# Causal attention on one core: the mask moves from TensorE products to the VectorE pass that takes the row maximum

## What is computed

```
q, kc, vc, ks, vs, kw, vw, gl = split(h @ w_in)      # 16 heads in 4 groups, head size 64
sc = q @ k_cmp.T ; p_c = softmax(where(valid_c, sc, -1e30))        # compressed keys (31)
ss = q @ ks.T    ; p_s = softmax(where(key_pos <= t_pos, ss, -1e30))  # selected blocks
sw = q @ kw.T    ; p_w = softmax(where(rel >= 0,         sw, -1e30))  # window of 512
o  = g0 * (p_c @ v_cmp) + g1 * (p_s @ vs) + g2 * (p_w @ vw)
out = o @ w_out
```

## Time and profile before

| | |
|---|---|
| time, median of 3 runs | 2454.04 us (2453.34 to 2454.38) |
| time of the profiled execution | 2452.17 us |
| span of the profiled execution | 2450.4 us, so 1.8 us lie around it |
| TensorE busy | 2412.6 us (98%) |
| VectorE busy | 1308.5 us (53%) |
| ScalarE busy | 884.7 us (36%) |
| TensorE clock granted | 0.996 of full speed |

### The profile page before, as it was taken

The page is one execution under the profiler, slowest core; times in us unless marked ns, Lnnn a source line. Parts: engine busy times, 40 slices in busy tenths (PEclk is TensorE's granted clock), DMA queues, the critical chain, the costliest instruction groups (busy, mean ns, idle before and its releaser), DMA issues.

```text
span 2450.4 us, 33828 instructions
## 1 busy us (share of the span) xinstructions
PE 2412.6 (98%) x12064; PEld 2015.1 (82%) x12064; DVE 1308.5 (53%) x1868; ACT 884.7 (36%) x1366; POOL 326.3 (13%) x314
## 2 busy tenths in 40 slices
PE   8999999999999999999999999999999999999998
PEld 6888888888888888888888888888888888888887
DVE  7656655444355655343487544446655665534444
ACT  5257753223234333222333322223336773322222
POOL 4311122000012030000033000003410114000003
PEclk9999999999999999999999999999999999999999
DMA  4810003232323223223232323233650002223232
GB/s 143 213 63 1 1 27 103 94 103 86 103 94 120 86 93 104 95 94 103 91 107 95 104 87 102 94 103 103 163 164 10 1 1 78 94 95 103 88 101 85
DMA packets 67480, 220.38 MB, mean 90 GB/s; under 512 B 7600, under 2 KB 11824, under 8 KB 67376
## 3 DMA queue, kind: packets, MB, share of 16 engines
q1 hardware_dynamic: 61680, 208.89, 25.8%
q0 software_dynamic: 5120, 8.39, 1.7%
q10 hardware_dynamic: 576, 1.69, 0.2%
HBM read 208.46 MB, written 2.10 MB: 86 GB/s over the span
## 4 chain that ended last, share of the span: by engine, by line
PE 93%; DVE 4%; ACT 1%; issue 1%; DMA 1%; DVEq 0%; SPq 0%; ACTq 0%
PE bank L1361 89%; PE bank L1583 3%; ACT attn L709 1%; DVE big L1260 1%; DVE w_lo L850 1%; DVE xs_lo L858 0%; DVE nmax L1098 0%; DMA raw<-stream 0%; ACT w_hi L525 0%; PE bank L1613 0%; DMA par<-params 0%; DVE big L1253 0%; DVE tmp L1221 0%; DVE big L1354 0%; DVE branch L1120 0%
## 5 line engine op out<-in xcount | busy, mean ns | idle before, releaser
L1361 PE MATMUL bank<-xs_hi,w_hi 128*128 128x512 f32 x1808 | 712.4, 394 | 7.4 <-DVE xs_lo L858 7.0
L1361 PE MATMUL bank<-xs_hi,w_lo 128*128 128x512 f32 x1808 | 704.6, 390 | 0.0
L1361 PE MATMUL bank<-xs_lo,w_hi 128*128 128x512 f32 x1808 | 704.5, 390 | 0.0
L850 DVE TENSOR_TENSOR w_lo<-raw,w_hi 128x1024 fp32r<-128x1024 f32 x372 | 471.2, 1270 | 242.8 <-ACT w_hi L525 238.4
L525 ACT ACTIVATE w_hi<-raw 128x1024 fp32r<-128x1024 f32 x373 | 391.8, 1051 | 432.1 <-PE bank L1361 257.2
L1361 PEld LDWEIGHTS bank<-xs_hi,w_hi 128*128 128x128 f32 x1808 | 339.9, 188 | 83.5 <-DVE xs_lo L858 8.1
L1361 PEld LDWEIGHTS bank<-xs_lo,w_hi 128*128 128x128 f32 x1808 | 340.1, 188 | 70.9 <-issue 1.9
L1361 PEld LDWEIGHTS bank<-xs_hi,w_lo 128*128 128x128 f32 x1808 | 339.9, 188 | 71.1
L1361 PE MATMUL bank<-hid_hi,w_hi 128*128 128x512 f32 x720 | 280.6, 390 | 0.0
L1361 PE MATMUL bank<-hid_lo,w_hi 128*128 128x512 f32 x720 | 280.1, 389 | 0.0
L1361 PE MATMUL bank<-hid_hi,w_lo 128*128 128x512 f32 x720 | 280.1, 389 | 0.0
(11 more groups left out here) (190 smaller groups left out, 2718.9 us busy)
## 6 DMA issues: line engine op xcount, KB each, us to landing
raw<-stream SPq DMA_DIRECT2D x371, 512.0 KB, 3.3
w_f<-stream SPq DMA_DIRECT2D x18, 512.0 KB, 4.0
hid_hi<-mix_hi POOLq DMA_DIRECT2D x32, 128.0 KB, 6.7
hid_lo<-mix_hi POOLq DMA_DIRECT2D x32, 128.0 KB, 6.7
x<-x_in SPq DMA_DIRECT2D x8, 256.0 KB, 8.6
out<-big SPq DMA_DIRECT2D x8, 256.0 KB, 3.5
raw<-stream ACTq DMA_DIRECT2D x2, 512.0 KB, 7.7
work<-b_s ACTq DMA_DIRECT2D x1, 512.0 KB, 5.0
```

Source lines behind the costliest of these rows:

```text
L850: nc.vector.tensor_tensor(w_lo[:, slot, :], raw[:, k, :], f32(w_hi[:, slot, :]), ALU.subtract).then_inc(w_lo_ready, counted(b))
L1361: return nc.tensor.matmul(out_, w, v, start=start, stop=stop)
```

## The change

The constant `causal_b` grows from 128 to 512 columns: 384 zeros and then the 128 by 128 triangle of -1e30, so that its last w columns are the mask of a unit of w columns. The mask products go. `maximum` of a causal pack becomes one instruction a unit that reads the scores from PSUM and the mask from SBUF, writes -(score + mask) to `prob` and takes its minimum, which is the negated maximum, into `nmax`. The exponents then read `prob` in place with scale -1. `scores(p)` waits for `max_ready` of pack p-2, no longer for its `prob_ready`. The wait for `prob_t` of pack p-4 moves from ScalarE to VectorE.

```diff
@@ exponents (ScalarE)
-                        wait_past(act, prob_t, p0 + p - 3)
                         for j in range(n):
-                            last = nc.scalar.activation(prob[:, p % 4, bass.ts(j, w)], bank[p % 2][:, bass.ts(j, w)],
-                                                        ACT.Exp, bias=nmax[:, p % 4, j:j + 1])
+                            sc = prob[:, p % 4, bass.ts(j, w)]
+                            last = nc.scalar.activation(sc, sc, ACT.Exp, bias=nmax[:, p % 4, j:j + 1], scale=-1.0)
@@ maximum (VectorE)
-                        sc = bank[p % 2][:, 0:pack_width(p)]
-                        nc.vector.tensor_reduce(nmax[:, p % 4, 0:n], sc.rearrange("p (j w) -> p j w", j=n), AX.X,
-                                                ALU.max, negate=True).then_inc(max_ready, 1)
+                        w = P * (t_of(i) + 1)
+                        wait_past(dve, prob_t, p0 + p - 3)
+                        for j in range(n):
+                            last = nc.vector.tensor_tensor_reduce(
+                                out=prob[:, p % 4, bass.ts(j, w)], in0=bank[p % 2][:, bass.ts(j, w)],
+                                in1=causal_b[:, S - w:S], scale=-1.0, scalar=-NEG, op0=ALU.add, op1=ALU.min,
+                                accum_out=nmax[:, p % 4, j:j + 1])
+                        last.then_inc(max_ready, 1)
@@ scores (TensorE)
-                    wait_past(pe, prob_ready, p0 + p - 1)
+                    wait_past(pe, max_ready, p0 + p - 1)
...
-                            mm(both, q, key_hi[:, :, g, 0:P], j == 0, False)
-                            mm(both, q, key_lo[:, :, g, 0:P], False, False)
-                        last = mm(dst[:, :].rearrange("p (k w) -> p k w", k=4), ident_b[:, :],
-                                  causal_b[:, :].unsqueeze(1).broadcast_to([P, 4, P]), False, True)
+                            mm(both, q, key_hi[:, :, g, 0:P], True, False)
+                            last = mm(both, q, key_lo[:, :, g, 0:P], False, True)
...
-                            mm(dst[:, bass.ts(k, w)], q, key_lo[:, br, g, 0:w], False, False)
-                            last = mm(dst[:, bass.ts(k * (t + 1) + t, P)], ident_b[:, :], causal_b[:, :], False, True)
+                            last = mm(dst[:, bass.ts(k, w)], q, key_lo[:, br, g, 0:w], False, True)
```

More of the change, by code:

```diff
@@ L85 @@
 PAR_COLS = _at
-CON = {"ident": 0, "causal": 128, "tril": 256, "cmask": 384, "end": 384 + TT * P}
+CON = {"ident": 0, "causal": P, "tril": P + S, "cmask": 2 * P + S, "end": 2 * P + S + TT * P}
 CON_COLS = CON["end"]
@@ L239, in build @@
         ident_b = sb("ident_b", [P, P], BF16)
-        causal_b = sb("causal_b", [P, P], BF16)
+        causal_b = sb("causal_b", [P, S], BF16)
         cmask_b = sb("cmask_b", [P, TT, P], BF16)
@@ L807, in _ @@
                                  ).then_inc(con_ready, 1)
-            nc.scalar.activation(causal_b[:, :], con[:, CON["causal"]:CON["causal"] + P], ACT.Copy
+            nc.scalar.activation(causal_b[:, :], con[:, CON["causal"]:CON["causal"] + S], ACT.Copy
                                  ).then_inc(con_ready, 1)
@@ L1840, in _consts @@
     con[:, CON["ident"]:CON["ident"] + P] = np.eye(P)
-    con[:, CON["causal"]:CON["causal"] + P] = np.where(r[None, :] > r[:, None], NEG, 0.0)
+    con[:, CON["causal"] + S - P:CON["causal"] + S] = np.where(r[None, :] > r[:, None], NEG, 0.0)
     con[:, CON["tril"]:CON["tril"] + P] = (r[None, :] >= r[:, None])
```

## The result

The changed kernel takes 2436.7 us (2435.5 to 2437.5, 4 runs) against 2453.7 before: ratio 0.9932, 95% interval 0.9915 to 0.995.

The account below looks back on a forecast made before the run. TensorE, busy 98% of the span, was taken to bound the kernel. Terms -13.8 (masks) + 2.4 (chain) + 0.6 (stall) + 2.8 (t1) = -8.0 us gave 2446.0 us, range 2440 to 2463.

Parts of the forecast that it names:

- a: VectorE's new fixed cost per unit, for the second instruction of a pass that writes `nmax`: taken as 0.08 us.
- the overlap: On VectorE, an instruction that waits for nothing starts 0.08 us before the end of the one before it.
- my lower bound of 0.013: Lowest fixed cost per unit considered, 0.013 us, from the companion instruction of the shuffle; the upper bound was 0.167.
- the 16 units: Units per group in which VectorE's fixed cost counts: 8 in the chain, one in the stall, about 7 others; 128 in all.
- my own formula: Sum of -8.0 us, moved by 1.3 us for each 0.01 us of fixed cost per unit; gain gone at 0.14.
- Masks: Mask products leaving TensorE: 7.7 us in t3 and t2 plus 6.1 in t1, so 13.8 us saved outside the chain.
- The chain at the group's end: Two t0 packs going round all three engines, TensorE waiting for exponents: 0.3 us longer, 2.4 us in 8 groups.
- The earlier wait: `scores` waits for `max_ready` alone, so its 0.6 us lie beside the exponents; otherwise the chain is 0.9 longer.
- The stall on `normalize_cs`: TensorE's wait for VectorE's normalization, some 6 us after the group's end: 0.08 us longer, 0.6 us in 8 groups.
- t1's loss of 0.35 a group: VectorE's extra 0.32 us in each of four t1 packs, a little over one showing: 0.35 a group, 2.8 us.
- The exponents from SBUF: ScalarE's exponents reading SBUF instead of PSUM: 0.03 us more an instruction, mattering for four in a row in t0.
- The rival that hung on the rule: Slower: no overlap between a pass and its second instruction, t0 units spaced 0.46 us, +14 us, 2468 us; chance 0.22.

Follow-up runs that it names:

- e2: Changed kernel with one more tiny VectorE copy of one column ahead of each of the 256 passes: 2447.48 us, ratio to before 0.9979.
- e3: Changed kernel with two tiny VectorE copies ahead of each pass: 2456.53 us, ratio to before 1.0021.
- e5: Kernel before without its mask products, nothing else changed, so its attention is not causal: 2438.15 us, ratio to before 0.9937.
- e1: Changed kernel with scores(p) waiting for `prob_ready` of pack p-2 again instead of `max_ready`: 2444.97 us, ratio to before 0.9963.
- e8: Changed kernel with both VectorE reorderings, `normalize_cs` of t0 items ahead of the maximum and `out_low` one step later: 2423.42 us, ratio to before 0.9884.
- e7: Changed kernel with `out_low` one step later on VectorE, behind the next maximum: 2429.82 us, ratio to before 0.9913.
- e6: Changed kernel with `normalize_cs` of the t0 items ahead of the maximum of the same step on VectorE: 2431.03 us, ratio to before 0.9921.
- e4: Changed kernel with the mask products put back on TensorE, so the mask is added twice: 2453.48 us, ratio to before 1.0012.

## Why the prediction was wrong

**The step that failed: "I take a = 0.08".** It was worked out as "0.167 - 0.08", a tiny pass less the overlap. Measured, a is 0.00 (the timeline above), below even my lower bound of 0.013. Two things were wrong in it. A tiny copy costs 0.06 where it stands ahead of each pass, not 0.08 (e2 and e3), which is a small matter. And the read of the accumulator is not like a tiny pass: it starts 0.08 us before the end of its own pass, and the next pass starts together with it, so that it delays nothing. I had taken one overlap off its duration, when it lies under its own pass as a whole.

**The size that this makes.** With the 13 units of e2 and e3, a = 0.08 would have made the group 43.48 + 13 x 0.08 = 44.5 us, an estimate, so 1.0 a group or 8 us in all below before: the forecast's 8.0. The sum came out right for the a that I put in, but in part by luck: the 16 units were too many, and the masks were worth more than I gave them (below). With a = 0 my own formula, -8.0 - 128 x 0.08, gives -18.2; with 13 units a group, 104 in all, -16.3. Measured are -16.3 by groups and -17.0 by the medians.

The group, cut at the chain's two ends (us, change against before; the e5 column has no mask and the old pass):

| part | forecast | changed | e5 |
|---|---|---|---|
| chain, last `lo` product of the first t0 pack to the transposes of the second | +0.30 | -0.25 | -0.24 |
| rest of the t3 item, with the stall | -0.40 | -0.48 | -0.64 |
| t2 item | -0.48 | -0.62 | -0.62 |
| t1 item | -0.41 | -0.76 | -0.58 |
| start of the t0 item to that `lo` product | 0 | +0.08 | 0 |
| sum | -0.99 | -2.03 | -2.08 |

Of the 1.04 us between forecast and measurement, the rows that hang on a (chain, rest of t3, t1) make up 0.55 + 0.08 + 0.35; the masks of the t2 item bring 0.14 more and the t0 start takes 0.08 back.

**Point by point.**
- Masks: forecast 13.8 us outside the chain, measured 16.6 in all (e5). In the timeline of the changed kernel the distance from the `lo` product to the transposes in t3 is what was forecast:

```profile
205.44 0.40 PE L1365 MATMUL bank<-hid_lo,mix_hi 128*128 128x512 f32 x1
205.68 0.38 PE L1584 MATMUL bank<-ident,attn 128*128 128x128 f32 x2
```

  0.24 us, against 0.30 before. Over a whole item a mask is worth a little more than these 0.06: t2's eight packs won 0.62, so 0.08 each. Of t1, 8.15 us became 7.39, so 0.19 for each of 4 packs, as forecast. Of t0's two masks the first one shortens the chain by its 0.23, which the forecast had in it (e5: 0.24). The second is not won: in e5 the chain is

```profile
194.87 0.28 PE L1361 MATMUL bank<-hid_lo,mix_hi 128*128 128x256 f32 x1
...
199.81 0.19 PEld L1361 LDWEIGHTS bank<-hid_hi,mix_hi 128*128 128x128 f32 x1 [0.94 <-ACT attn L709]
...
200.38 0.60 PE L1580 MATMUL bank<-ident,attn 128*128 128x128 f32 x4
```

  5.51 us against 5.75, and TensorE's wait for the exponents grew from 0.70 to 0.94. To leave t0's masks out of the sum and in the chain was right.
- The chain at the group's end: forecast 0.3 us longer. From the last `lo` product of the first t0 pack to the transposes of the second it was 5.75 us (195.41 to 201.16) and is 5.50 (191.72 to 197.22), so 0.25 shorter; with 8 x 0.08 less for a the forecast's 0.3 is -0.34. The working was right, a again was not.
- The earlier wait: forecast 0.6 us a group in the chain, measured 0.57 there and 0.59 in the group (e1), with a part in t1 that was not forecast.
- The stall on `normalize_cs`: forecast 0.1 longer by a, measured 1.49 against 1.47.
- t1's loss of 0.35 a group: not there at a = 0, and too large for a = 0.08 as well. How it would have come is in e2: t1 7.39 to 7.44, t0 5.32 to 5.50, t3 17.91 to 18.46; in e3 t1 is 7.57, so 0.18 longer at 0.12 us a unit. Most of the cost of a larger a falls into t0 and t3, where the chain lies.
- The exponents from SBUF: +0.03 an instruction forecast, +0.035 measured.
- The rule that the next operation starts only when the pipeline is empty (the Trainium skill, VectorE: DVE Perf Modes, The DRAIN you can't avoid) does not hold for the rows of the pair: both the read and the next pass start 0.08 us before the pass ends. The same section goes on to say that a next operation that is not held starts earlier, which the prediction left out; the rows here fit that exception. The rival that hung on the rule, 2468 us, falls.

The chances had 0.50 on faster, but the range was too short at its lower end. It was said to take in a from 0.02 on and to end at 2440, while the formula of the same text gives 2438.3 at a = 0.02 and 2435.8 at a = 0. A lower bound of nothing for the read would have had the measured time inside.

## What to carry to other kernels

A VectorE pass that also gives a row result is listed as two instructions, but price it by the start-to-start spacing of such rows, not by the sum of the durations. Here work was moved from the engine that bounds to one with a third of its time free. That paid in full where VectorE is ahead, and added VectorE time cost something mainly in the few steps in which the work goes round through all engines (13 of 32 units in e2 and e3). And a stall in a fixed order is worth a look of its own: two moves in VectorE's list gave nearly as much (e8: 1.78 us a group, 14 us) as the change itself (2.04 a group, 16 us).

## What was not expected of the hardware

The granted TensorE clock differs between runs of one kernel, and the time with it. In one group of e3 the windows show (columns as in the earlier trace rows):

```profile
241.00:264.00 23.00, 20.38 (x122) 17.47 (x120) 14.01 (x68) 13.03 (x29) 2.76 (x4) 0.78 0.00 1
264.00:309.00 45.00, 41.94 (x338) 39.00 (x337) 33.89 (x177) 33.40 (x75) 5.82 (x8) 1.00 0.01 1
```

The mean clock was 0.78 there, so a part of that stretch ran at the lower of the two levels (1.2 against 2.4 GHz), and the t3 item took 22.9 us where its neighbours took 19.0. A second t3 item of the same run, in the other attention layer, took 22.8. These two hold 7.7 of the 14 us by which the profiled run (2462.3 us) lies above what its groups give.

Most traces here have a stretch of lower clock in the first group of an attention layer, of different length from trace to trace. In the kernel before it comes after TensorE was busy for only 2.90 us of a stretch of 5:

```profile
155.00:160.00 5.00, 2.90 (x14) 1.48 (x13) 3.74 (x7) 2.03 (x4) 0.00 (x0) 0.86 0.00 0
160.00:165.00 5.00, 5.00 (x24) 4.48 (x24) 1.38 (x2) 1.44 (x3) 0.00 (x0) 0.50 0.00 0
```

The t3 item of a first group took from 19.8 to 23.7 us in the traces here; it is at 19.8 or 19.9 in both layers of e2 and e7.

Over whole runs, a lower mean clock goes with a longer time of the same kernel. In e1 it was 0.992 to 0.995, and its time went from 2448.3 us at the lowest to 2441.5 at the highest. Its two runs at 0.995 took 2441.5 and 2441.6 us, which is the 2441.4 that its group gives. In e3 it was 0.987 to 0.993, with 2466 to 2454 us. Its groups say 3.7 us faster than before, and it was 4.5 slower in the same series.

Whether the waits brought the lower clock is not shown. For it: e3, with the most VectorE time added, has the lowest clock, and e7 and e8, with fewer and shorter waits than the changed kernel (0.994 to 0.996), have 0.995 to 0.998. Against it: e6 has shorter waits too and is at 0.993 to 0.995, and e4, whose group is as long as before, has two runs at 0.99 among others at 0.995 to 0.998. And a stretch like the one ahead of e3's fall (240 to 245 us, TensorE busy 3.59 of 5) kept the full clock in the changed kernel (200 to 205 us, busy 3.51). What share of each run's excess the clock has was not separated by a run of its own.
